# Output weights loaded from ScalarE's queue, and VectorE's routing tables in three parts

## What is computed

```python
out_c = attention(q, k, v)                               # 8 heads, 96 wide; 1024 queries on 1280 keys
mixed = jnp.concatenate([out_a, out_b, out_c], axis=-1)  # 256 + 256 + 512 = 1024
mix   = jnp.einsum('bnm,md->bnd', mixed, P['w_out'][l])
x = x + g1 * mix
h = rmsnorm(x, P['norm2_g'][l]) * (1 + sc2) + sh2
x = x + g2 * ec_ffn(h, P['w_router'][l], ...)            # 16 experts: router softmax, top 128 tokens each, SwiGLU
```

## Time and profile before

| | us |
|---|---|
| median of three runs | 1523.24 |
| lowest, highest | 1519.10, 1527.53 |
| the profiled execution, its own time | 1522.13 |
| its span, first to last instruction | 1520.2 |
| PE busy in that span | 1480.5 (97%) |
| DVE, ACT, POOL busy | 605.1, 408.0, 280.3 |

### The profile page before, as it was taken

One profiled execution on the slowest core, in us unless ns is written; L12 is line 12 of the kernel. 1 busy time (PEld: TensorE's weight loads), 2 busy tenths in 40 slices (PEclk: granted clock), 3 DMA queues, 4 the chain that ended last, 5 costly groups with the idle time before them and its releaser, 6 DMA issues.

```text
span 1520.2 us, 25562 instructions
## 1 busy us (share of the span) xinstructions
PE 1480.5 (97%) x10145; PEld 1180.3 (78%) x10145; DVE 605.1 (40%) x1385; ACT 408.0 (27%) x933; POOL 280.3 (18%) x308
## 2 busy tenths in 40 slices
PE   6999999999999999999999999999999999999997
PEld 3654545666666655444899999999999999999996
DVE  2211446676868673136683222222222222222215
ACT  2400102555646452235321111111111111111114
POOL 0005400463747463110000100100000000000000
PEclk9999999999999999999999999999999999999999
DMA  9971001475747593541587999999889989899885
GB/s 364 353 261 50 32 0 41 82 137 104 142 98 144 130 200 73 194 166 70 191 322 271 323 294 312 315 353 300 291 316 296 362 293 300 313 292 357 291 260 223
DMA packets 313917, 338.79 MB, mean 223 GB/s; under 512 B 209091, under 2 KB 210666, under 8 KB 311678
## 3 DMA queue, kind: packets, MB, share of 16 engines
q1 hardware_dynamic: 308814, 319.58, 66.4%
q0 software_dynamic: 4752, 17.30, 4.4%
q10 hardware_dynamic: 288, 1.05, 0.2%
HBM read 266.18 MB, written 21.64 MB: 189 GB/s over the span
## 4 chain that ended last, share of the span: by engine, by line
PE 88%; DVE 5%; DMA 4%; ACT 2%; issue 1%; POOL 0%; SPq 0%; DVEq 0%; ACTq 0%; POOLq 0%
PE ps L1286 32%; PE ps L1315 16%; PE ps L678 8%; PE ps L1016 7%; PE ps L915 6%; PE ps L969 4%; DMA wreg<-wreg 2%; PE ps L703 2%; PE ps L869 2%; PE ps L693 1%; PE ps L894 1%; PE ps L881 1%; DVE stat L1921 1%; PE ps L710 1%; DMA wreg<-x_rows 1%
## 5 line engine op out<-in xcount | busy, mean ns | idle before, releaser
L1286 PE MATMUL ps<-mreg,wreg 128*128 128x144 f32 x4096 | 506.3, 286 | 0.0
L1286 PEld LDWEIGHTS ps<-mreg,wreg 128*128 128x128 f32 x4096 | 503.4, 190 | 0.7 <-ACT hreg L1625 0.4
L1315 PE MATMUL ps<-mreg,wreg 128*128 128x144 f32 x2048 | 256.4, 286 | 2.1 <-DVE mreg L2365 2.1
L1315 PEld LDWEIGHTS ps<-mreg,wreg 128*128 128x128 f32 x2048 | 253.1, 190 | 2.5 <-DVE mreg L2365 2.3
L2365 DVE TENSOR_TENSOR mreg<-ps,mreg 128x144 f32<-128x144 f32 x128 | 39.4, 307 | 357.6 <-PE ps L1286 346.7
L2530 POOL COPY wreg<-hreg 128x1024 uint16<-128x1024 uint16 x128 | 146.2, 1168 | 156.7 <-ACT hreg L1504 156.1
L915 PE MATMUL ps<-wreg 128*128 128x512 f32 (+2 forms) x400 | 159.0, 520 | 3.8 <-ACT hreg L1504 3.7
L1662 ACT ACTIVATE mreg<-ps 128x144 f32<-128x144 f32 x128 | 37.2, 291 | 426.1 <-PE ps L1286 426.1
L1016 PE MATMUL ps<-wreg,mreg 128*128 128x512 f32 x288 | 130.5, 598 | 0.0
L678 PE MATMUL ps<-hreg,wreg 128*128 128x512 f32 (+1 forms) x400 | 128.9, 480 | 0.0
L2577 POOL DMA_INDIRECT x_rows<-hreg,idx_s x15 | 23.9, 1596 | 533.1 <-DVE hreg L2342 521.6
(11 more groups left out here) (310 smaller groups left out, 1217.7 us busy)
## 6 DMA issues: line engine op xcount, KB each, us to landing
wreg<-in_w_e_dram SPq DMA_DIRECT2D x96, 2048.0 KB, 12.4
wreg<-in_w_ada_dram SPq DMA_DIRECT2D x16, 1024.0 KB, 8.3
wreg<-in_w_ada_dram SPq DMA_DIRECT2D x16, 512.0 KB, 10.9
wreg<-in_w_out_dram SPq DMA_DIRECT2D x8, 512.0 KB, 4.2
wreg<-in_x_sample_dram SPq DMA_DIRECT2D x8, 512.0 KB, 4.6
x_rows<-wreg SPq DMA_DIRECT2D x8, 512.0 KB, 3.5
xn_rows<-wreg SPq DMA_DIRECT2D x8, 512.0 KB, 2.6
wreg<-x_rows SPq DMA_DIRECT2D x8, 512.0 KB, 8.5
```

What stands on the lines that cost most here:

```text
L1286: mm = pe.matmul(o[:, 0:CAP], w[s][:, k, (f % 4) * P:(f % 4 + 1) * P], xsT[b][:, k, :], start=(k == 0), stop=(k == KD - 1))
L1315: mm = pe.matmul(bank[4 + dm % 2][:, 0:CAP], w2[f // 4][:, f % 4, dm * P:(dm + 1) * P], hidT[:, f, :], start=(f == 0), stop=(f == 7))
```

## The change

On SP, the eight loads of `w_out` leave the loop over n. On ACT, the fourth pass (`attend(3, True)`) issues them instead: behind the exponential of n = 2, 4, 6 and 8, two loads each, the first of them behind a wait for `q_moved`. On DVE, `routing_tables()` is cut in three: the scaled matrix of the sample behind the trip of n = 6, that of the prompt behind the trip of n = 8 (`scaled_router`), the rest behind the trip of n = 10. Work and bytes are the same.

```diff
             for n in range(16):
                 turn_prob(3, n)
-                if n < KD:
-                    sp.dma_start(w_out_sb[:, n, :], w_out[0, n * P:(n + 1) * P, :]).then_inc(w_out_in, 16)
...
-            def attend(i):
+            def attend(i, last=False):
...
                     exponential(n)
+                    if last and n < 10:
+                        if n == 2:
+                            act.wait_ge(q_moved, 4 * 64)
+                        for k in (n - 2, n - 1):
+                            act.dma_start(w_out_sb[:, k, :], w_out[0, k * P:(k + 1) * P, :]).then_inc(w_out_in, 16)
                     turned(n - 1, 2)
...
-            attend(3)
+            attend(3, True)
...
-                    elif n == 6:
+                    elif not more and n == 6:
+                        scaled_router(0)
+                    elif not more and n == 8:
+                        scaled_router(1)
+                    elif not more and n == 10:
                         routing_tables()
...
-            def routing_tables():
-
+            def scaled_router(cnd):
                 dve.wait_ge(proj_mm, 36)
                 dve.wait_ge(gain_ok, 3)
                 dve.wait_ge(small_in, 16 * 10)
-                for cnd in range(2):
-                    ins = dve.tensor_tensor(w_rs[:, cnd, :, :], w_r[:], gain2[:, cnd, :].unsqueeze(2).to_broadcast([P, KD, 32]),
-                                            ALU.mult)
+                dve.tensor_tensor(w_rs[:, cnd, :, :], w_r[:], gain2[:, cnd, :].unsqueeze(2).to_broadcast([P, KD, 32]),
+                                  ALU.mult)
+
+            def routing_tables():
+
```

## The result

The changed kernel takes 1531.44 us in the median of 7 runs (1529.99 to 1536.66), the kernel before 1522.25 in the median of 7 (1518.93 to 1527.53): a ratio of 1.0061, 95% interval 1.0046 to 1.0076. It is 9.2 us slower, where 1.5 was forecast. The forecast was 1524.7 with a range up to 1530.0; the time lies outside it, half a microsecond above the rival "the loads go first, whole" (1530.9).

A forecast was written before the change was run, and what follows sets the result against it. The prediction took the fourth pass to be bound by full DMAs delaying transposes. Its terms, 0 + 0 + 0 + (6.5 - 5.0) = +1.5 us, on the median of 1523.24 gave 1524.7 us, range 1517.5 to 1530.

The forecast's parts named there:

- the loads go first, whole: Rival: each pair of loads stands in front of an odd query's first half; +7.7 us, 1530.9; chance 0.17.
- The fourth pass is bound by its DMAs, and the trip has no slack for a late transpose: Fourth pass: DMAs full, no engine short; 0.13 us spare in a trip of 7.49 us.
- The fourth pass loses 5.0 us: Fourth pass takes 57.46 us against the third's 52.46; 5.0 us is the most the change can win back.
- What is lost there reaches the end one for one: Behind the fourth pass PE is busy for 32.80 of 33 us, so gains or losses reach the end in full.
- SP's and ACT's issues at 0: SP losing eight load issues (4.6 us of queue) and ACT gaining eight (0.9 us a pair) each change the time by 0.
- The tables at 0: DVE's 2.4 us block of routing tables, cut in three, fits DVE's idle 0.82 us a trip; cost 0.
- The loads' place: Pairs of loads beside odd queries' transposes: 2.0 us each at three trips, 0.5 at n = 2; 6.5 lost instead of 5.0.
- The prediction's last sign: Sign of the forecast being wrong in another way: a transpose's landing held until the other queue is empty; no size given.
- Nothing moves: Rival: full DMAs, same bytes and engines, so 5.0 us are lost again; 0, 1523.2 us; chance 0.13.

The follow-up runs named there:

- e4: Changed kernel without the output weights' loads and the output matmuls' wait for them, tables in three parts; fourth pass 54.03 us, one run.
- e2: Changed kernel with the loads back on SP, one behind each n = 0 to 7, tables in three parts; fourth pass 57.34 us, ratio to before 1.0004.
- e11: e6 with the routing tables in one block at n = 6; fourth pass 53.75 us, ratio to the kernel before 0.9981.
- after: The changed kernel itself, two loads on ACT's queue behind n = 2, 4, 6, 8; fourth pass 66.97 us, ratio to the kernel before 1.0061.
- e1: Changed kernel with the routing tables in one block at n = 6 again; fourth pass 67.67 us, ratio to the kernel before 1.0067.
- e8: Changed kernel with the load of flip_sb moved from behind n = 1 to behind n = 9 on SP; fourth pass 69.73 us, one run.
- e13: Changed kernel with each load on ACT's queue split into two halves of 2 KB a row; fourth pass 69.92 us, one run.
- e7: Changed kernel with the pairs of loads on ACT's queue behind n = 4, 6, 8, 10 instead; fourth pass 69.88 us, one run.
- e6: Changed kernel with all eight loads on ACT's queue ahead of the fourth pass; fourth pass 53.14 us, ratio to the kernel before 0.9978.
- e3: Changed kernel with the pairs of loads on SP's queue, behind the transposes of n = 2, 4, 6, 8; fourth pass 57.67 us, ratio to before 1.0009.
- e14: Changed kernel with all eight loads in one go on ACT's queue behind the exponential of n = 8; fourth pass 67.51 us, one run.

## Why the prediction was wrong, point by point

*The fourth pass is bound by its DMAs, and the trip has no slack for a late transpose:* right. The four waits of PE follow four late transposes in the chain, and where the loads are gone, 0.7 us is the longest wait that is left (e4).

*"The fourth pass loses 5.0 us", the most that can be won:* right as a bound, but 1.6 of it are lost without any load in e4's execution. 3.7 to 4.3 could be won.

*What is lost there reaches the end one for one:* right. 9.5 us in the pass, 9.2 in the medians.

*SP's and ACT's issues at 0:* nothing speaks against it. ACT's DMA issue runs beside the exponential; the row at 521.37 lies inside that at 521.36. What did grow is SP's issue of a transpose, to 5.9 us in a collision, and no term had that. *The tables at 0:* right (e2, e11).

*The loads' place:* **this is the step that failed.** For n = 2 it had 0.5 us, on the ground that the odd query's first half was nearly through, and it is 6.5, and 1.2 more in the next trip, mostly at the lower clock. That half was nearly through (ACT waits 0.62 us for it), but it was not the one that counted: the second transpose of n = 1, which DVE joins, was issued 0.1 us behind the first load and shared the engines with the two of them. Second halves of odd queries are what stands in the chain all four times; the prediction gave the trip's slack for the first halves alone. For the pairs of n = 4, 6 and 8 it had 2.0 us each. That of n = 4 makes PE wait nowhere for over 1 us, those of 6 and 8 for 2.62 and 2.49: 5.1 us for 6.0, the right size in sum. The 1.14 us behind them had no load in flight. With 0.5 in place of the 6.5 and 1.2 the pass would have taken 66.97 - 7.2 = 59.8 us, not far from the forecast of 52.5 + 6.5 = 59.0. No run lets one say beforehand which collision will be the dear one: it was at n = 2 in three kernels (after, e1, e8), at n = 8 in e13 and at n = 10 in e7.

How 2.0 was found was the weaker part. It took the landing of transposes with one load ahead of them *in their own line* for the nearest row and doubled it. The 3.9 us for two loads are too long as well: 271 GB/s is from a stretch with a DMA share of 0.83, while with the engines full (e6, the row above) 3.13 MB move in 8 us, 391 GB/s, so that two loads take 2.7 us. A load in line is paid once, by whatever stands behind it, and the gaps of a DMA share of 0.72 absorb most of it: two in line cost no more than one (e3, 57.67 against 57.46). A load on a second queue is not in line. The rival "the loads go first, whole" had that right, with the packet-by-packet rule behind it. That its time, 1530.9, is nearest to the result is luck in good part: it had 1.0 at n = 2 and 3.9 for each later pair, where 6.5 and at most 2.9 a trip were measured, and turns by packet explain some 2.5 of the 7.0 us by which the first transpose was late. The prediction's last sign, a landing held until the other queue is empty, describes that one better: it came at 531.6, and the second load landed at 531.4. The rival had a chance of 0.17, half of which was counted as slower; the range ended below it.

"Nothing moves" rested on the full DMA share: same bytes, same engines, same time. The share of 1.06 with 136 GB/s shows why that is no argument: a full engine says nothing about whose packets it serves. That issuing from another engine saves only issue time (the Trainium skill, the same page, Issuing engines are not separate DMA queues) does not hold for this kernel: from after to e3, which has the same pairs behind the same queries on SP's queue, the pass falls by 9.3 us.

**What stays open** is what makes some packets of either queue take up to 2 us in some collisions (43 of 256 rows of weights over 0.32 us in the first of the changed kernel) and none for 5 us on end in another (e14, 554 to 559 us). In e8's first, with `flip_sb` out of it, the rows for 523 to 534 us give means of 35 and 260 ns at the same medians, so it is not `flip_sb`; and smaller packets do not cure it (e13). The rows of e8:

```profile
q1 hardware_dynamic: 3662, 0.91, 71.9%
q10 hardware_dynamic: 288, 1.05, 42.6%
```

## What to carry to other kernels

Before moving a bulk load to another queue, look for small, urgent transfers that run at the same time on the first one. In one queue they take turns transfer by transfer, and on two queues packet by packet (505 to 505 in e14), so packets of 4 KB win against the transposes' of 250 bytes (2.74 MB in 11066); ask which urgent transfer is under way when the load starts. The better place for such a load is a stretch in which the DMA share is near 0; here one lay 10 us ahead of the pass, and the trace of the kernel before shows it.

## What the runs showed of the hardware

- Two busy DMA queues were served the same number of packets (505 and 505 in 5 us of e14), though one had packets of 4 KB and the other of 256 bytes: the first had 90.6% of the engines' time, the second 11.4%.
- In the first collision of the changed kernel single packets took up to 2.2 us (1.0 at most in the kernel before, 524 to 532 us) where the median stayed at 159 ns, and from 525 to 531 us the engines moved 136 GB/s at a share of 1.06; in the same stretch of the kernel before, with one queue, they moved 274 GB/s at 1.07.
- Halved packets took about half the time: 86 ns in the median for 2 KB (e13, 549 to 556 us), 159 for 4 KB.
- A 16 KB packet of the instruction queue took 0.9 to 1.0 us of one engine in e4. Each of the three transposes that landed there in 4.7 to 4.9 us instead of 3.1 to 3.5 had one in its flight; that the packet was the reason was not tested.
- A wait of 5.4 us cost PE its clock for 6.8 us, with products at half speed after the wait had ended. In e7 the `weigh` group behind a wait of 2.58 us ran slowly (3.29 us, clock 0.57 from 538 to 542 us), the one behind 2.62 in the changed kernel did not (1.97, clock 1.00).
- ACT issues a DMA 10 ns after the activation ahead of it in program order has begun: "behind the exponential" means beside it.
